# Two token groups on either side of three RMS norms in a two-block transformer kernel

## The reference, cut to what matters

```python
def rms_norm(x, w):
    xf = x.astype(jnp.float32)
    y = xf * lax.rsqrt(jnp.mean(xf * xf, axis=-1, keepdims=True) + EPS)
    return (y * w.astype(jnp.float32)).astype(x.dtype)
...
        x = x + token_mixer(h, w_in[l], ...)
        h = rms_norm(x, ffn_norm_w[l])
        x = x + conv_ffn(h, w_up[l], conv_w[l], conv_b[l], w_down[l])
```

## Time and profile before

| | |
|---|---|
| median of 3 runs | 2057.66 us (2057.37 to 2057.93) |
| profiled execution, its own time | 2083.68 us |
| span of the profile | 2081.9 us |
| mean granted clock of PE | 0.911 |
| busy share of PE, DVE, ACT | 88%, 49%, 37% |

### The profile page before, as it was taken

The page is one execution under the profiler, slowest core; times in us unless marked ns, Lnnn a source line. Parts: engine busy times, 40 slices in busy tenths (PEclk is TensorE's granted clock), DMA queues, the critical chain, the costliest instruction groups (busy, mean ns, idle before and its releaser), DMA issues.

```text
span 2081.9 us, 23598 instructions
## 1 busy us (share of the span) xinstructions
PE 1836.1 (88%) x8490; PEld 1468.6 (71%) x8490; DVE 1011.6 (49%) x1635; ACT 775.6 (37%) x1358; POOL 70.0 (3%) x90
## 2 busy tenths in 40 slices
PE   5897699999989799998988978988996997798987
PEld 4787577777767688886867875657884666677966
DVE  5234466666444565563234335565364234535654
ACT  3122144444332455552132125444154352315651
POOL 0000012000000000000000000000000000000001
PEclk8789599999999899999999998787997898898998
DMA  7321001111234133332222230010321011111111
GB/s 182 90 61 41 1 11 61 61 56 50 93 101 131 51 101 101 92 87 80 96 75 81 86 101 1 21 41 21 116 62 61 21 41 47 61 61 41 42 41 41
DMA packets 155316, 135.74 MB, mean 65 GB/s; under 512 B 9616, under 2 KB 150800, under 8 KB 155104
## 3 DMA queue, kind: packets, MB, share of 16 engines
q1 hardware_dynamic: 150656, 121.35, 19.7%
q0 software_dynamic: 3136, 10.78, 1.5%
q10 hardware_dynamic: 1440, 2.50, 0.4%
HBM read 127.28 MB, written 7.34 MB: 65 GB/s over the span
## 4 chain that ended last, share of the span: by engine, by line
PE 79%; DVE 12%; issue 4%; ACT 3%; DMA 1%; SPq 1%; DVEq 0%; POOL 0%; ACTq 0%
PE bank L294 18%; PE bank L296 18%; PE bank L295 18%; PE bank L1018 3%; PE bank L989 2%; PE bank L1002 2%; DVE wlo L287 1%; PE bank L883 1%; ACT whi L280 1%; PE bank L476 1%; PE bank L2484 1%; PE bank L2120 1%; DVE ssn L443 1%; PE bank L1668 1%; PE bank L1666 1%
## 5 line engine op out<-in xcount | busy, mean ns | idle before, releaser
L294 PE MATMUL bank<-hh,whi 128*128 128x512 f32 (+2 forms) x1104 | 452.5, 410 | 37.0 <-DVE hl L415 20.1
L295 PE MATMUL bank<-hl,whi 128*128 128x512 f32 (+2 forms) x1104 | 441.7, 400 | 0.0
L296 PE MATMUL bank<-hh,wlo 128*128 128x512 f32 (+2 forms) x1104 | 441.0, 399 | 0.0
L280 ACT ACTIVATE whi<-wraw 128x2048 fp32r<-128x2048 f32 x112 | 213.9, 1911 | 396.0 <-PE bank L296 392.6
L287 DVE TENSOR_TENSOR wlo<-wraw,whi 128x2048 fp32r<-128x2048 f32 x112 | 256.3, 2289 | 197.8 <-ACT whi L280 196.4
L294 PEld LDWEIGHTS bank<-hh,whi 128*128 128x128 f32 (+2 forms) x1104 | 212.4, 192 | 98.9 <-issue 25.7
L296 PEld LDWEIGHTS bank<-hh,wlo 128*128 128x128 f32 (+2 forms) x1104 | 212.6, 193 | 48.6
L295 PEld LDWEIGHTS bank<-hl,whi 128*128 128x128 f32 (+2 forms) x1104 | 213.3, 193 | 43.6 <-issue 1.7
L1042 DVE COPY pt<-bank 128x128 f32<-128x128 f32 (+2 forms) x96 | 42.6, 469 | 104.4 <-PE bank L1002 104.4
L294 PE MATMUL bank<-ah,whi 128*128 128x512 f32 x192 | 77.1, 401 | 12.0 <-DVE al L2619 8.5
L1052 ACT ACTIVATE pr<-bank,nm 128x128 f32<-128x128 f32 (+3 forms) x128 | 66.2, 529 | 46.5 <-DVE nm L1113 46.4
(11 more groups left out here) (360 smaller groups left out, 3116.4 us busy)
## 6 DMA issues: line engine op xcount, KB each, us to landing
wraw<-in_w_in_a_dram SPq DMA_DIRECT2D x52, 512.0 KB, 4.5
wraw<-in_w_up_dram SPq DMA_DIRECT2D x42, 512.0 KB, 4.8
wraw<-in_w_in_dram SPq DMA_DIRECT2D x34, 512.0 KB, 4.7
wraw<-in_w_in_c_dram SPq DMA_DIRECT2D x18, 512.0 KB, 4.3
wraw<-in_w_down_dram SPq DMA_DIRECT2D x16, 512.0 KB, 4.3
wraw<-in_w_out_a_dram SPq DMA_DIRECT2D x16, 512.0 KB, 4.3
aside<-stage POOLq DMA_DIRECT2D x20, 256.0 KB, 2.3
w<-in_cmp_w_dram SPq DMA_DIRECT2D x4, 1024.0 KB, 12.6
```

The lines of the kernel that those rows point to most:

```text
L280: act.activation(whi[:, p], wraw[:, p], ACT.Copy).then_inc(w_hi_done, 1)
L294: pe.matmul(out, ws[0], hs[0], start=first, stop=False)
L295: pe.matmul(out, ws[0], hs[1], start=False, stop=False)
L296: return pe.matmul(out, ws[1], hs[0], start=False, stop=last)
```

## The change

The 512 tokens are cut into two halves of 256 (h = 0, 1) on both sides of each of the three norms. In front of the norm the last tiles of the residual stage (four in `residual_norm`, two in `ffn_down`) are computed for half 0 first, then for half 1 in other banks; each pass there has 256 tokens instead of 512, and there are two of them. The two partition sums of half 0 stand behind the first half-1 tile, the spreading behind the second. Behind the norm the next stage's first four tiles are computed for half 0, then for half 1 (`halved_items`), and the small matmuls of half 1's norm stand between the half-0 tiles. The wait of PE for all evictions (`pe.wait_ge(drained, m0)`) at that stage's start is gone. DVE and ACT handle half 0's norm, the evictions of half 1 and the splits of the next items in one new order (`HalfNorm`). Before norm 3 the next stage was `window_kv` and then `project`; now it is half of `project` (four tiles), `window_kv`, and the other half of `project`. Loops of two turns in these stages are written out.

```diff
+    def half_tile(pe, b, t, out, rhs, h, kts=KT, k0=0, first=True, last=True, ready=None):
+        p, cs, ts = b % 2, slice(P * t, P * t + P), token_half(h)
+        for k in range(kts):
+            if ready:
+                pe.wait_ge(ready[0], ready[1] + k + 1)
+            mm = passes(pe, out[:, ts], (whi[:, p, k, cs], wlo[:, p, k, cs]),
+                        (rhs[0][:, k0 + k, ts], rhs[1][:, k0 + k, ts]), first and k == 0, last and k == kts - 1)
+        return mm
+    def halved_items(pe, b, ready, between):
+        for h in range(2):
+            for t in range(4):
+                if h == 0 and t % 2 == 0:
+                    item_ready(pe, b + t // 2)
+                mm = half_tile(pe, b + t // 2, t % 2, bank[t], H, h,
+                               ready=(ready[0], ready[1] + KT * h) if t == 0 else None)
+                if h:
+                    mm.then_inc(tiles, 1)
+                elif t < 2:
+                    between[t](pe)
...
+        def square(self, act, k, h):
+            ts = slice(0, S) if k < self.f else token_half(h)
+            if k < self.f or h:
+                act.wait_ge(drained, self.m0 + k + 1)
+            else:
+                act.wait_ge(half_drained, self.c["half"] + k - self.f + 1)
+            act.wait_ge(n_add, self.place(k - 2, h if k - 2 >= self.f else 0) if k >= 2 else self.c["add"])
+            act.activation(sqn[:, k % 2, ts], xt[:, k, ts], ACT.Square).then_inc(n_sq, 1)
+        def root(self, act, h):
+            act.wait_ge(n_sum, self.c["sum"] + h + 1)
+            act.activation(rtn[:, 2 * h:2 * h + 2], bank[(self.a, self.b)[h]][:, 0:2], ACT.Sqrt,
+                           bias=eps[:, self.eps_col:self.eps_col + 1], scale=1.0 / D).then_inc(n_inv, 1)
...
+        def scalar(self, act):
+            f = self.f
+            for k in range(f, KT):
+                self.square(act, k, 0)
+            self.root(act, 0)
+            split_hi(act, self.next_item)
+            for k in range(KT):
+                if f == 4 and k in (1, 3, 5):
+                    self.square(act, f + k // 2, 1)
+                self.high(act, k, 0)
+            for k in range(KT - 1 if f == 4 else f, KT):
+                self.square(act, k, 1)
+            split_hi(act, self.next_item + 1)
+            self.root(act, 1)
+            for k in range(KT):
+                self.high(act, k, 1)
...
+        def evict(self, dve, k, h, t_done):
+            ts = token_half(h)
+            if h:
+                dve.wait_ge(tiles, t_done)
+            else:
+                dve.wait_ge(half_tiles, self.c["half"] + k - self.f + 1)
+            out = bank[(self.b if h else self.a) + k - self.f]
+            dve.tensor_tensor(xt[:, k, ts], xt[:, k, ts], out[:, ts], ALU.add) \
+                .then_inc(drained if h else half_drained, 1)
...
+        def vector(self, dve, t_done):
+            f = self.f
+            for k in range(f, KT):
+                self.evict(dve, k, 0, None)
+                if k > f:
+                    self.add(dve, k - 1, 0)
+            self.add(dve, KT - 1, 0)
+            self.inverse(dve, 0)
+            dve.wait_ge(n_spread, self.c["spread"] + 1)
+            for k in range(KT):
+                self.full(dve, k, 0)
+                if f == 4 and k in (0, 2, 4):
+                    self.evict(dve, f + k // 2, 1, t_done(f + k // 2))
+                if k:
+                    self.low(dve, k - 1, 0)
+                if f == 4 and k in (2, 4, 6):
+                    self.add(dve, f + k // 2 - 1, 1)
+                if k == 3:
+                    split_lo(dve, self.next_item)
+            self.low(dve, KT - 1, 0)
+            for k in range(KT - 1 if f == 4 else f, KT):
+                self.evict(dve, k, 1, t_done(k))
+                self.add(dve, k, 1)
+            split_lo(dve, self.next_item + 1)
+            self.inverse(dve, 1)
+            dve.wait_ge(n_spread, self.c["spread"] + 2)
+            for k in range(KT):
+                self.full(dve, k, 1)
+                if k:
+                    self.low(dve, k - 1, 1)
+            self.low(dve, KT - 1, 1)
+        def sums(self, pe, h):
+            pe.wait_ge(n_add, self.place(KT - 1, h))
+            for t in range(2):
+                mm = pe.matmul(bank[(self.a, self.b)[h]][:, t:t + 1], ssn[:, HS * h + P * t:HS * h + P * t + P],
+                               ones[:, 0:1], start=True, stop=True)
+            mm.then_inc(n_sum, 1)
+        def spread(self, pe, h):
+            pe.wait_ge(n_inv, self.c["inv"] + 2 * h + 2)
+            out = bank[(self.a, self.b)[h] + 1]
+            for t in range(2 * h, 2 * h + 2):
+                mm = pe.matmul(out[:, P * t:P * t + P], rrn[:, t:t + 1].to_broadcast([P, P]), ident[:, :],
+                               start=True, stop=True)
+            mm.then_inc(n_spread, 1)
...
+    def residual_norm(mat, rhs, weight, eps_col, r0=0, ready=None):
+        n0, m0 = new_items(4), new_tiles(KT)
+        nrm = HalfNorm(m0, 4, weight, eps_col, (0, 4), n0 + 4)
...
+        @block.tensor
+        def _(pe):
+            pe.wait_ge(drained, m0)
+            for t in range(4):
+                if t % 2 == 0:
+                    item_ready(pe, n0 + t // 2)
+                tile_of(pe, n0 + t // 2, t % 2, bank[t][:, :], rhs, ready=ready if t == 0 else None) \
+                    .then_inc(tiles, 1)
+            for t in range(4):
+                b = n0 + 2 + t // 2
+                if t % 2 == 0:
+                    item_ready(pe, b)
+                pe.wait_ge(drained, m0 + t + 1)
+                half_tile(pe, b, t % 2, bank[t], rhs, 0).then_inc(half_tiles, 1)
+            for t in range(4):
+                half_tile(pe, n0 + 2 + t // 2, t % 2, bank[4 + t], rhs, 1).then_inc(tiles, 1)
+                if t == 0:
+                    nrm.sums(pe, 0)
+                if t == 1:
+                    nrm.spread(pe, 0)
+        @block.scalar
+        def _(act):
+            split_hi(act, n0 + 2)
+            split_hi(act, n0 + 3)
+            for k in range(4):
+                nrm.square(act, k, 0)
+            nrm.scalar(act)
...
-            pe.wait_ge(drained, m0)
-            each(None, pe, lambda b, j, i, f, n: products(pe, b, j, i, f, n))
+            halved_items(pe, n0, ready, between)
+            each(1, pe, lambda b, j, i, f, n: products(pe, b, j, i, f, n))
...
+            item_ready(pe, n0 + PER * (MI - 1))
+            for h in range(2):
+                for t in range(2):
+                    if h == 0:
+                        pe.wait_ge(drained, m0 + 2 + t + 1)
+                    mm = halved(0, t, h)
+                    if h:
+                        mm.then_inc(tiles, 1)
+            for part in range(1, PER):
+                item_ready(pe, n0 + PER * (MI - 1) + part)
+                for t in range(2):
+                    mm = halved(part, t, 0)
+                    if part == PER - 1:
+                        mm.then_inc(half_tiles, 1)
+            for part in range(1, PER):
+                for t in range(2):
+                    halved(part, t, 1).then_inc(tiles, 1)
+                    if part == 1:
+                        (nrm.spread if t else nrm.sums)(pe, 0)
         def _(act):
-            for j in range(PER * MI - 1):
-                split_hi(act, n0 + 2 + j)
+            for j in range(2, PER * MI - 1):
+                split_hi(act, n0 + j)
+            for k in range(6):
+                nrm.square(act, k, 0)
+            split_hi(act, n0 + PER * MI - 1)
+            nrm.scalar(act)
...
+            if not ready:
+                pe.wait_ge(drained, m0 + 4 * parts[0])
+            for i in parts:
+                if ready and i == 0:
+                    halved_items(pe, n0, ready, between)
+                    continue
...
-    mx = residual(w["w_o"], (mh, ml), ready=ready, late=True)
-    ffn_up(norm(mx, "ffn_norm", 0, late=count["item"] + 1))
-    mx = ffn_down()
+    ffn_up(*residual_norm(w["w_o"], (mh, ml), "ffn_norm", 0, ready=ready))
     wa = w["w_in_a_2"]
-    project(wa, 0, q2, SCALE, ready=norm(mx, "norm_a", 1, late=count["item"] + 1))
+    ready, between = ffn_down("norm_a", 1)
...
-    mx = residual(w["w_out_a_2"], (bh, bl), r0=D, ready=ssd_norm(), late=True)
-    window_kv(norm(mx, "norm_c", 1, late=count["item"] + 1))
-    m1 = project(w["w_in_c_2"], 0, q3, SCALE, bias="b_q") + KT
+    ready, between = residual_norm(w["w_out_a_2"], (bh, bl), "norm_c", 1, r0=D, ready=ssd_norm())
+    project(w["w_in_c_2"], 0, q3, SCALE, bias="b_q", ready=ready, between=between, parts=(0,))
+    window_kv()
+    m1 = project(w["w_in_c_2"], 0, q3, SCALE, bias="b_q", parts=(1,)) + KT
```

More of the change, by code:

```diff
@@ L406, in two_blocks, with norm @@
     norms = [0]
-    def norm(m0, weight, eps_col, late=None):
+    def norm(m0, weight, eps_col):
         c = norms[0]
@@ L1279, in block1_merge, with residual @@
         return (g_low, AHEAD)
-    def residual(mat, rhs, r0=0, last=False, ready=None, late=False):
```

(26 more changed lines are left out.)

182 lines of the change are left out of this document (119 added, 63 removed).

## The result

The changed kernel takes 2043.31 us (median of 7 runs, 2040.79 to 2046.82). The kernel before took 2060.93 us beside it (7 runs, 2057.37 to 2069.83). The ratio is 0.9908, interval 0.9884 to 0.9931: 0.7 to 1.2% faster, 14 to 24 us. The profiled execution took 2046.82 us; its span is 2045.0 us and PE's mean granted clock 0.925 (0.911 before).

What follows compares the result with a forecast made beforehand. PE's passes bound the kernel, apart from serial chains at three norms. A full-clock gain of 23.8 us less 4.1 for the clock gave 19.7, so 2057.66 became 2038 us; range 2030 to 2051, likeliest case 2036 to 2043.

Steps and rivals of the forecast that it cites:

- The stall is what the change reaches: At each of three norms PE loses 19.7 us to a serial chain; 59 us is all the change can reach.
- The walk at norms 1 and 3: Last whole tile to next stage's fourth tile: 53.7 us instead of 63.2, with 4.9 us of waits; 9.5 us gained each.
- The small matmuls: Sums and spreading now stand among passes and cost 2.2 us a norm; the other bound was 4.0 us.
- DVE's pairs of halves: DVE and ACT on 256 columns: a pair of halves costs 0.15 us more than the whole instruction.
- rival C: DVE is the next bound, 3 us more a norm; gain 6 to 15 us, time 2043 to 2052; chance 0.17.
- Norm 2: `wlo` 1.6 us late, `hl` 1.3, sums 2.2, spreading 0.4: waits 5.4 us, and 8.0 us gained.
- What comes behind: Costs after the norms: 2.0 us waiting once in `ffn_up`, and 1.2 us for one added barrier from moving `window_kv`.
- The barrier: At the next stage's start, dropping PE's wait for evictions itself gives nothing, since the `hl` wait is later.
- The sum: All three norms at full clock: 9.5 + 8.0 + 9.5 - 2.0 - 1.2 = 23.8 us gained.
- The clock: Short waits following each other lower PE's clock: 1.4 us charged a norm, 4.1 in all; bounds 0 and twice that.
- Rival A: The forecast: waits as walked and one clock drop at each norm; gain 15 to 21 us, 2036 to 2043; chance 0.45.
- rival B: No clock drop, or low only where PE waits anyway; gain 21 to 28 us, 2030 to 2036; chance 0.25.

Runs made afterwards that it cites:

- after: The changed kernel in its first runs and profile, against the kernel before: 2043.31 us, ratio 0.9908.
- after again: The changed kernel with no edit, timed and profiled a second time: 2046.73 us, ratio 0.9899 to the kernel before.
- none: The changed kernel's unrolled loops with no halves at any norm and the barriers kept: 2063.52 us, ratio 0.9991 to the kernel before.
- only1: Halves at norm 1 alone, norms 2 and 3 as in the kernel before: 2059.57 us, ratio 0.9955 to the kernel before.
- fillers: Changed kernel with useless small matmuls issued where PE waits at each norm: 2040.04 us, ratio 0.9879; with DVE's `wlo` also ahead of the gate's product in `ffn_up`, 2034.91 us.
- lofirst: Changed kernel with DVE making the next `wlo` ahead of the gate's product in `ffn_up`: 2051.43 us, ratio 0.9887 to the kernel before.

## Why the prediction was right, point by point

**The stall is what the change reaches.** Right. Span less clock is 1967.8 to 1968.1 us with no halves and 1941.8 to 1946.9 in the seven profiles with halves at three norms and no barrier. With the norm stages taken off too, the same two groups have 1499.1 to 1502.1 and 1499.2 to 1502.8 us: what moves is the norm stages.

**The walk at norms 1 and 3** (53.7 us; waits 1.4, 2.2, 0.9 and 0.4). Measured 52.65 us; `wlo` 1.08, `hl` 1.10, sums 0.62, spreading 0.16. Places and order were right, and the sum of waits was too high by 1.9 us. Most of that went elsewhere, into a price that the prediction put at nothing. Around the first wait in the timeline above, from the last pass (693.26) to the first one behind the wait (694.62) are 1.36 us, of which 1.08 are the wait, 0.12 the usual pace and 0.16 neither; and from there to the next pass are 0.22 us instead of 0.12 (694.84, 694.96). So a wait costs about 0.26 us more than its idle time, some 1.6 us for six. The small matmuls took 0.50 + 0.60 + 0.61 + 0.71 = 2.4 us, where 2.2 were charged; the prediction's other bound for them, 4.0 us, would have made 3 x 1.8 = 5.4 us in all and not the 2.5 that it names. Gained were 10.6 instead of 9.5 us up to the fourth tile.

The walk also comes out at more than its own terms. Sixteen half tiles of 2.875 us, 2.2 of small matmuls and 4.9 of waits are 53.1 us, not 53.7, and so 10.1 us gained.

**DVE's pairs of halves** (0.15 us dearer than a whole one). DVE's timeline of the kernel after, half 1, first normed tiles:

```profile
705.92 0.42 DVE L595 TENSOR_TENSOR hl<-hfn,hh 128x256 fp32r<-128x256 f32 x1
706.38 0.48 DVE L588 SCALAR_TENSOR_TENSOR hfn<-xt,parm,bank 128x256 f32<-128x256 f32 x1
706.78 0.42 DVE L595 TENSOR_TENSOR hl<-hfn,hh 128x256 fp32r<-128x256 f32 x1
707.23 0.48 DVE L588 SCALAR_TENSOR_TENSOR hfn<-xt,parm,bank 128x256 f32<-128x256 f32 x1
```

0.42 and 0.48 us, and 0.85 a k (706.38 to 707.23), as taken from the rows of that width. With that rival C (DVE bound, 2043 to 2052) lost its price, although the median landed on its edge. "VectorE: DVE Perf Modes" of the Trainium skill, section "The TRN2 errata", advises 512 elements or more. The fixed part is there in the rows (0.15 us a pair); how much of it lay under PE's passes and how much in the 2.96 us of waits, no run here separates.

**Norm 2** (8.0). With the clock at 1.00 (after again) 72.4 became 63.5: 8.9. The waits were 1.42, 0.45 and 1.86 (predicted 1.6, 1.3, 2.2). Here too the recorded gain is less than its terms give: 19.7 less 2.9 for 228 halved passes, 2.2 and 5.4 is 9.1.

**What comes behind.** The wait at `ffn_up`'s third item: 2.0 predicted, 2.02 measured. The barrier at `window_kv`: 1.2 predicted, 0.94 measured. At norm 3, 9.5 - 1.2 = 8.3 were predicted; 106.6 (none and only1) to 98.5 is 8.1. That agreement is partly luck, because the clock was at half behind `window_kv` in every profile with norm 3 halved, for 3.4 to 6.8 us, and at 1.00 there in none and only1. PE's timeline and a window of the kernel after:

```profile
1818.73 0.80 PE L294 MATMUL bank<-hh,whi 128*128 128x512 f32 x1 [3.41 <-DVE vp L2668]
```

```profile
1818.30:1822.00 3.70, 3.27 (x8) 2.62 (x9) 1.65 (x5) 0.00 (x0) 0.00 (x0) 0.54 0.67 213
```

The first seven passes behind this wait took 3.14 us from start to start, and 1.74 in none: 1.4 us lost. Without it norm 3 would have gained 9.5 us. The two profiles of before had the fall too (6.8 and 3.4 us at half; the stage took 109.6 and 108.6). The prediction counted none of this.

**The barrier.** "Dropping PE's barrier itself gives nothing" is true of the old order, where `hl` comes later. In the new order it is false: there the barrier would stand behind half 1's evictions, and with it PE waits 6.02 us at norm 1 instead of 2.96.

**The sum** at full clock was 23.8 us. The stages show 8.4 + 8.9 + 8.1 = 25.4, or 26.8 with the 1.4 us behind `window_kv` put back. By the prediction's own terms it should have read 10.1 + 9.1 + 10.1 - 2.0 - 1.2 = 26.1.

**The clock** (1.4 us at each norm, 4.1 in all). Near as a mean and wrong as a description. A norm's train loses nothing, or 1.7 us of PE's passes (clock at half for 3.4 us), or 3.2 to 3.4 us (twice as long). Over the nine norms of the three profiles without fillers the ledger's loss is 1.7 + 5.0 + 8.3 = 15.0 us; 1.7 of it stands behind the third item of `ffn_up`, so the trains lost 13.3, 4.4 a run. In the length of the stages, which is how the 1.4 us was measured, it was less: 1.1, 3.8 and 4.6 us, 3.2 a run. Rival A (a drop at each norm) is true of lofirst, rival B (none) nearly of after: they were never two cases but two draws. The Trainium skill's rule ("TensorE: Matmul & The Clock Gate", "A second HAM failure mode: psum-queue depth-cycling") has the direction that the fillers speak for, not the certainty that I took from it. PE's idle time was also overrated: 4.5 of 7.6 us by the walk, 2.6 of 8.0 in the window above.

**The time.** 2057.66 - 19.7 = 2038 was forecast; 2043.31 came out, within the range, outside the likeliest case's own 2036 to 2043 by 0.3. The kernel before, run beside it, took 2060.93 and not 2057.66: 3.3 of the 5.3 us are that. The other 2.0 lie within the interval: the gain was 19.7 by forecast, 17.6 in the first set of runs and 21.7 in the second. The step that was loose is the base: I had three runs within 0.6 us, and carried the profiled execution's 26 us along as a fixed difference. It was one draw of a wide spread: 23 runs beside the first experiments lay between 2056.95 and 2085.59. So the mechanism was right, and that the time came so near is in part luck: waits that were too long stood against a price of each wait that was left out, and a sum too low at full clock against a fall behind `window_kv` that nobody had counted.

## What to carry to other kernels

Where a reduction stands between two dense stages, and one token's result needs no other token, cut the tokens in two on both sides and let the second half's passes cover the first half's chain. Halving a 512-column pass cost 0.013 us here. Check that the halved vector work fits under the other half's passes, and take away the barrier on the last evictions, which would have cost 5 to 11.5 us of the gain. Fill the short waits that are left with matmuls nobody reads: here they cost nothing that the stages show, and the clock never fell behind them. Price a wait above its idle time (0.26 us more here). When a few us matter, compare profiles stage by stage with the clock's share taken off, and not by their spans; and run the versions that you compare beside each other.

## What the runs showed of the hardware

The same train of six short waits at norm 1 let the clock fall in one execution (after again) and not in another (after). In the kernel before the clock was at half for 13.7 to 17.1 us at every norm; at norm 1 PE was busy for 10.2 of the 16 us from 696 to 712. Two profiles of one kernel differ by 18.5 us (113.9 and 95.4) in time lost to the clock in stages where nothing was changed. Of the five falls behind a train in after, after again and lofirst, two cost 1.7 us of PE's passes and three 3.2 to 3.4; the pass pace at half clock was 0.21 us for 256 columns, against 0.12 (after, norm 2). A wait cost PE about 0.26 us beyond its idle time (after, 693.26 to 694.96).
